# The weight sums of a seven-product matrix multiply: from VectorE to transfers that add

## The reference, cut to what matters

```
h = rms_norm(x, norm_ffn)
gate, up = jnp.split(h @ w_gate_up, 2, axis=-1)      # 1024 -> 2 x 2816
x = x + (jax.nn.silu(gate) * up) @ w_down            # 2816 -> 1024
```

## Time and profile before

| | us |
|---|---|
| median of three runs | 1362.07 |
| lowest and highest | 1361.05, 1362.75 |
| the profiled execution, its own time | 1360.11 |
| its span in the trace | 1358.3 |

### The profile page before, as it was taken

How to read it: one execution, slowest core, us unless ns; L and a number is a source line. 1 busy time by engine, 2 the same in 40 slices (tenths; PEclk the granted TensorE clock), 3 DMA queues, 4 the chain that set the end, 5 groups by cost and what they waited for, 6 DMA issues and landing times. The chain is left out here.

```text
span 1358.3 us, 18018 instructions
## 1 busy us (share of the span) xinstructions
PE 1339.5 (99%) x6941; PEld 1112.0 (82%) x6941; DVE 849.2 (63%) x1313; ACT 619.4 (46%) x1145; POOL 54.1 (4%) x38
## 2 busy tenths in 40 slices
PE   9999999999999999999999999999999999999998
PEld 7888878888888888888788887888798888888886
DVE  5785654457666554344558876767565666666668
ACT  6554333457777533223426466663343332433333
POOL 0025300000000000000010000000000000000000
PEclk9999999999999999999999999999999999999999
DMA  5222213242111154322261200002325412421321
GB/s 168 86 83 81 67 59 114 88 138 80 36 59 61 63 188 151 104 91 66 87 195 61 70 17 16 32 1 78 130 88 168 142 38 87 154 94 63 113 73 62
DMA packets 33622, 120.68 MB, mean 89 GB/s; under 512 B 3716, under 2 KB 5124, under 8 KB 32258
## 3 DMA queue, kind: packets, MB, share of 16 engines
q1 hardware_dynamic: 32962, 118.48, 26.3%
q10 hardware_dynamic: 576, 1.05, 0.4%
HBM read 112.18 MB, written 4.19 MB: 86 GB/s over the span
## 5 line engine op out<-in xcount | busy, mean ns | idle before, releaser
L983 PE MATMUL bank<-a_hi,whi 128*128 128x512 f32 (+1 forms) x880 | 346.9, 394 | 0.4 <-DVE a_lo L2381 0.4
L983 PE MATMUL bank<-a_hi,wlo 128*128 128x512 f32 (+1 forms) x880 | 337.1, 383 | 0.0
L983 PE MATMUL bank<-a_lo,whi 128*128 128x512 f32 (+1 forms) x880 | 336.2, 382 | 0.0
L1431 ACT ACTIVATE whi<-wraw 128x1024 fp32r<-128x1024 f32 x170 | 176.0, 1055 | 195.6 <-PE bank L983 135.1
L1808 DVE TENSOR_TENSOR wlo<-wraw,whi 128x1024 fp32r<-128x1024 f32 x170 | 207.6, 1234 | 60.7 <-ACT whi L1431 54.7
L983 PEld LDWEIGHTS bank<-a_hi,wlo 128*128 128x128 f32 x880 | 165.5, 188 | 32.7
L983 PEld LDWEIGHTS bank<-a_hi,whi 128*128 128x128 f32 x880 | 165.9, 189 | 31.6 <-issue 2.3
L983 PEld LDWEIGHTS bank<-a_lo,whi 128*128 128x128 f32 x880 | 165.9, 189 | 31.1 <-issue 1.7
L983 PE MATMUL bank<-arena 128*128 128x128 f32 (+5 forms) x1332 | 184.9, 284 | 3.0 <-DVE arena L2032 1.5
L983 PEld LDWEIGHTS bank<-arena 128*128 128x128 f32 (+1 forms) x1332 | 163.9, 190 | 13.0 <-issue 5.3
L983 PE MATMUL bank<-whi,a_hi 128*128 128x512 f32 x288 | 115.6, 401 | 1.5 <-DVE wlo L1808 0.7
(11 more groups left out here) (272 smaller groups left out, 1866.5 us busy)
## 6 DMA issues: line engine op xcount, KB each, us to landing
wraw<-in_wblk SPq DMA_DIRECT2D x170, 512.0 KB, 3.8
arena<-in_quarters SPq DMA_DIRECT2D x8, 1024.0 KB, 7.1
arena<-in_quarters SPq DMA_DIRECT2D x4, 768.0 KB, 6.1
arena<-in_x SPq DMA_DIRECT2D x4, 512.0 KB, 6.1
arena<-in_x SPq DMA_DIRECT2D x1, 2048.0 KB, 7.7
spill<-arena SPq DMA_DIRECT2D x4, 512.0 KB, 7.8
arena<-spill SPq DMA_DIRECT2D x1, 2048.0 KB, 9.3
out<-arena SPq DMA_DIRECT2D x8, 256.0 KB, 2.0
```

What stands on the lines that cost most here:

```text
L983: return nc.tensor.matmul(o, lhsT, rhs, start=start, stop=stop, **kw)
L1431: A(whi[n % 2][:, cols], wraw[i][:, 0:cols.stop - cols.start], ACT.Copy).then_inc(s_hi, 1)
```

## The change

The scheme's signs are chosen anew, so that all four weight sums are plain sums: t1 = b11 + b12, t2 = b11 + b12 + b22, t3 = b12 + b22, t4 = t2 + b21. None is made on VectorE. SP copies one quarter into the sum's slot, and POOL issues transfers that add further quarters from HBM onto it: t1 one, t3 one, t2 two, the second after the first has landed. t4 has no slot of its own: b21 is added onto t2 in place, after both rests of product 6 have been made. There are six copies and five adds per group, 33 transfers of quarters where there were 12. The slots are b11 (later b22), b21, t2 (later t4), t1, t3. The copies go ahead of ff 4 (t2), 5 (t1, t3), 6 (b11), 7 (b21) in group 0, the same places of ff 12 to 15 in group 1, and ahead of ff 19 (t2, t1), 20 (t3, b11), 21 (b21) in group 2. b22 goes ahead of the second woven block of the next group (for the last group, after all block weights), and waits for the rests of product 1. From the second group on, the others wait for the rests of the product of the group before that used the slot last; for t2 that is product 4. In the hidden sums two operations change sign, and two takes subtract in place of one.

```diff
@@ -72,9 +72,11 @@
 PRODUCT_ORDER = (1, 2, 6, 5, 7, 3, 4)
 CONTINUES = (6, 7, 3)
 PAIR = {1: 0, 6: 0, 7: 0, 4: 0, 2: 1, 5: 1, 3: 1}
+SUBTRACTED = {(6, (0, 1)), (7, (1, 1))}
 TAKES = {1: ((0, 0),), 2: ((0, 0),), 6: ((0, 1),), 5: ((1, 1),), 7: ((1, 0), (1, 1)), 3: ((0, 1),), 4: ((1, 0),)}
-QUARTERS = ("b11", "b12", "b21", "b22")
-SUMS = ("t1", "t2", "t3", "t4")
+QUARTERS = ("b11", "b21", "b22", "t1", "t3", "t2")
+COPIED = {"b11": 0, "b21": 2, "b22": 3, "t1": 0, "t3": 1, "t2": 0}
+ADDED = {"t1": (1,), "t3": (3,), "t2": (1, 3)}
@@ -291,17 +293,14 @@
         woven = group + 1 < len(FFP)
         for c in range(max(a + 3 * (group > 0), 2), e):
             f = ff(c, a, whole)
-            sums = [("tsum", group, 0)] if c == e - 2 else []
-            steps += f[:2] + untaken + H(*unsplit) + f[2:4] + sums + f[4:]
+            steps += f[:2] + untaken + H(*unsplit) + f[2:]
             untaken, unsplit = [], [c]
-        steps[-2:-2] = [("tsum", group, 1)]
         made = products(group, (e - a) // 2)
         for p in PRODUCT_ORDER:
             m = next(made)
             if p == 1 and not woven:
                 untaken, unsplit = H(*unsplit), []
-            sums = {6: [("tsum", group, 2)], 7: [("tsum", group, 3)]}.get(p, [])
-            steps += m[:2] + untaken + m[2:-1] + sums + m[-1:]
+            steps += m[:2] + untaken + m[2:]
             untaken = [("take", m[0][1])]
             if woven and p in (1, 6, 7):
                 c = FFP[group + 1][0] + (1, 6, 7).index(p)
@@ -575,12 +574,16 @@
 OUT1 = sorted((g for g, (kind, _) in enumerate(TILES) if kind == "out1"), key=DONE.get)
 LATE = min(n for n, b in enumerate(BLOCKS) if TILES[b["tiles"][0]][0] == "z_sb") + 1
 LOADED = [n for n, b in enumerate(BLOCKS) if b["form"] != "product"]
-LAST_OF = {"b12": 7, "b22": 3, "b21": 4}
+LAST_OF = {"t1": 5, "t3": 7, "b11": 3, "b21": 2, "t2": 4}
 QUARTERS_AT = {}
 for group, (a, e) in enumerate(FFP):
-    for c, name in zip(range(e - 4, e) if e - a == 8 else (e - 3, e - 3, e - 2, e - 1), ("b11", "b12", "b22", "b21")):
+    for c, name in zip((e - 4, e - 3, e - 3, e - 2, e - 1) if e - a == 8 else (e - 3, e - 3, e - 2, e - 2, e - 1),
+                       ("t2", "t1", "t3", "b11", "b21")):
         n = next(n for n, b in enumerate(BLOCKS) if TILES[b["tiles"][0]] == ("ff_gate", (c, c - a)))
         QUARTERS_AT.setdefault(n, []).append((group, name))
+    if group + 1 < len(FFP):
+        n = next(n for n, b in enumerate(BLOCKS) if TILES[b["tiles"][0]] == ("ff_gate", (e + 1, 1)))
+        QUARTERS_AT.setdefault(n, []).append((group, "b22"))
 PRODUCT_AT = {(b["group"], b["product"]): n for n, b in enumerate(BLOCKS) if b["form"] == "product"}
 MERGE_AFTER = max(n for n, b in enumerate(BLOCKS) if b["w"] == "gate_sb")
 TURNS = [s for s in SPLITS if s[0] in ("turn", "nsa", "chunk")]
@@ -756,8 +759,8 @@
         hsq = mem(4, [512])
-        raw = {name: mem(kb, [BLK]) for name, kb in (("b11", 0), ("b12", 8), ("b21", 16), ("b22", 24), ("t1", 32))}
-        raw.update(t2=raw["b11"], t3=raw["b12"], t4=raw["b21"])
+        raw = {name: mem(kb, [BLK]) for name, kb in (("b11", 0), ("b21", 8), ("t2", 16), ("t1", 24), ("t3", 32))}
+        raw.update(b22=raw["b11"], t4=raw["t2"])
         half_chunk = T // 2
         first_hi, first_lo = [mem(kb, [4, half_chunk], rounded_arena) for kb in (40, 44)]
         other_hi, other_lo = [mem(kb, [2, 4, half_chunk], rounded_arena) for kb in (52, 60)]
@@ -841,7 +844,7 @@
         s_qk2, s_k2 = sem("s_nsa_stacks_rounded"), sem("s_nsa_keys_twice")
         s_kcl = sem("s_kc_rest")
         s_raw = {name: sem("s_quarter_" + name) for name in QUARTERS}
-        s_tsum = sem("s_weights_summed")
+        s_added = {name: sem("s_quarter_added_" + name) for name in (*ADDED, "t4")}
         s_h, s_hsum, s_hround = sem("s_hidden_made"), sem("s_hidden_summed"), sem("s_hidden_rounded")
         s_hlb, s_hlev = sem("s_lower"), sem("s_hgrn_operands")
@@ -901,6 +904,20 @@
         @block.sync
         def _(sp):
             by_token = lambda ap: ap.rearrange("(a p) d -> p a d", p=P)
+            def load_quarter(group, name):
+                if name == "b22":
+                    sp.wait_ge(s_lo, 2 * PRODUCT_AT[group, 1] + 2)
+                elif group == 0:
+                    sp.wait_ge(s_norm, norm_no("ffn", NT - 1))
+                    sp.wait_ge(s_split, max(SPLITS.index(x) for x in SPLITS if x[:2] == ("turn", "ffn")) + 1)
+                else:
+                    sp.wait_ge(s_lo, 2 * PRODUCT_AT[group - 1, LAST_OF[name]] + 2)
+                cols = slice(0, width(PRODUCT_AT[group, 1]))
+                src = dram["quarters"][4 * group + COPIED[name]]
+                sp.dma_start(raw[name][:, cols], src[:, cols]).then_inc(s_raw[name], 16)
             for t in range(NT):
                 if t == 1:
                     sp.dma_start(cst[:, :], dram["cst"]).then_inc(s_ident, 16)
@@ -908,16 +925,7 @@
             sp.dma_start(swraw[:, 0:NK * SH], dram["w_dt"]).then_inc(s_sw, 16)
             for at, n in enumerate(LOADED):
                 for group, name in QUARTERS_AT.get(n, ()):
-                    if group == 0:
-                        sp.wait_ge(s_norm, norm_no("ffn", NT - 1))
-                        sp.wait_ge(s_split, max(SPLITS.index(x) for x in SPLITS if x[:2] == ("turn", "ffn")) + 1)
-                    elif name == "b11":
-                        sp.wait_ge(s_tsum, len(SUMS) * group)
-                    else:
-                        sp.wait_ge(s_lo, 2 * PRODUCT_AT[group - 1, LAST_OF[name]] + 2)
-                    cols = slice(0, width(PRODUCT_AT[group, 1]))
-                    src = dram["quarters"][len(QUARTERS) * group + QUARTERS.index(name)]
-                    sp.dma_start(raw[name][:, cols], src[:, cols]).then_inc(s_raw[name], 16)
+                    load_quarter(group, name)
                 for i in range(2):
                     if n >= 1:
                         sp.wait_ge(s_lo, 2 * LOADED[at - 1] + i + 1)
@@ -969,6 +977,7 @@
                     sp.wait_ge(s_spill, 16 * NT)
                     sp.dma_start(x2, by_token(spill)).then_inc(s_back, 16)
                     sp.dma_start(rows["ffn"], dram["norm_ffn"]).then_inc(s_row["ffn"], 16)
+            load_quarter(len(FFP) - 1, "b22")
             for p, (rows_half, cols_half) in ((2, (0, 0)), (7, (1, 1)), (3, (0, 1)), (4, (1, 0))):
                 for t in range(2):
                     sp.wait_ge(*ended(tile_of("down", (len(FFP) - 1, p, t))))
@@ -1421,10 +1430,10 @@
                 cols = piece(n, i)
                 if BLOCKS[n]["form"] == "product":
                     group, name = BLOCKS[n]["group"], PRODUCTS_OF[BLOCKS[n]["product"]][1]
-                    if name in QUARTERS:
+                    if name in COPIED and name not in ADDED:
                         act.wait_ge(s_raw[name], 16 * group + 16)
                     else:
-                        act.wait_ge(s_tsum, len(SUMS) * group + SUMS.index(name) + 1)
+                        act.wait_ge(s_added[name], 16 * len(ADDED.get(name, "1")) * (group + 1))
                     A(whi[n % 2][:, cols], raw[name][:, cols], ACT.Copy).then_inc(s_hi, 1)
                     return
                 act.wait_ge(s_w[i], 16 * (LOADED.index(n) + 1))
@@ -1949,32 +1958,14 @@
                 a12, a22 = h[:, 0:half_chunk], h[:, half_chunk:T]
                 dve.wait_ge(s_h, c + 1)
                 v.tensor_tensor(hsum[:, 2, :], a11, a21, ALU.subtract)
-                link(v.tensor_tensor(hsum[:, 0, :], a21, a22, ALU.add))
+                link(v.tensor_tensor(hsum[:, 0, :], a21, a22, ALU.subtract))
                 link(v.tensor_tensor(hsum[:, 1, :], hsum[:, 0, :], a11, ALU.subtract))
-                v.tensor_tensor(hsum[:, 3, :], a12, hsum[:, 1, :], ALU.subtract).then_inc(s_hsum, 1)
+                v.tensor_tensor(hsum[:, 3, :], a12, hsum[:, 1, :], ALU.add).then_inc(s_hsum, 1)
                 dve.wait_ge(s_hround, rounded_of_h(c) - 1)
                 v.tensor_tensor(other_lo[:, :, pair, :], h.rearrange("p (a b) -> p a b", b=half_chunk),
                                 f32(other_hi[:, :, pair, :]), ALU.subtract).then_inc(s_split, 1)
                 dve.wait_ge(s_hround, rounded_of_h(c))
                 v.tensor_tensor(sums_lo[:, :, pair, :], hsum, f32(sums_hi[:, :, pair, :]), ALU.subtract).then_inc(s_split, 1)
-
-            def tsum(group, i):
-
-                cols = slice(0, width(PRODUCT_AT[group, 1]))
-                r = {name: ap[:, cols] for name, ap in raw.items()}
-                out_, left, right = (("t1", "b12", "b11"), ("t2", "b22", "t1"), ("t3", "b22", "b12"), ("t4", "t2", "b21"))[i]
-                for name in (left, right):
-                    if name in QUARTERS:
-                        dve.wait_ge(s_raw[name], 16 * group + 16)
-                    else:
-                        dve.wait_ge(s_tsum, len(SUMS) * group + SUMS.index(name) + 1)
-                if out_ == "t3":
-                    dve.wait_ge(s_tsum, len(SUMS) * group + 1)
```

(28 more changed lines are left out.)

## The result

The changed kernel takes 1386.8 us (median of four runs, 1384.5 to 1387.2) against 1361.6 for the kernel before (1359.7 to 1362.8, four runs beside it): ratio 1.0185, 95% interval 1.0172 to 1.0198. It is 25 us slower. The forecast was 1366.9, with a range up to 1380: the right sign, a fifth of the size.

What follows compares the result with a forecast made beforehand. TensorE was taken as the bound, busy 1339.5 of 1358.3 us. Block 19's wait 3.55, first add 0.8, block 20 0.5, less 0.1 gained, made +4.8 us on the 1362.07 median: 1366.9 us, range 1364.5 to 1380.

Steps and rivals of the forecast that it cites:

- The bound and the gain: Whole kernel: TensorE bounds it; removing twelve VectorE sums (25.3 us) gains 0.1 us, at most 2.0 us.
- The pause near 1328: Last group, before the matmul at 1329.85: 1.9 us, caused by the hidden split after block 21, not the sums; stays.
- The wait for product 4 in front of block 19: Group 2, SP's queue: t2's wait for product 4's last rest delays block 19's weights; stall 3.55 us.
- The 0.8 us for the first add: Group 2, block 19: t2's first add slows the first weight piece; 0.8 us taken, bounds 0 to 2.5 us.
- hidden, with little to spare: Group 0, weights up to block 6: copies 18.4 us plus four adds 13.4 us fill 32 of 34 us; no stall.
- Group 1's "hidden": Group 1: t2's copy waits until about 1158, before block 12's weights, issued 1162.25 and wanted at 1176; no stall.
- rival 2: SP's queue: adds cost 5.0 us each and starve weights; 16.4 us in group 2, up to 11 each in groups 0, 1; chance 0.24.
- Weights must land 2.5 us before: Group 0, block 6 beginning near 1073: its weights must land some 2.5 us before its start.
- Blocks 20 and 21: Group 2 after block 19: block 20 stalls 0.5 us, bounds 0 to 2.8; block 21 has a whole block more.
- The margin of 2.2 us for block 20: Group 2: block 20's first piece lands at 1300.7, wanted at 1302.9, against up to two adds of 2.5 us each.
- 2.45 us from landing to start: Feed-forward blocks 19 and 20: 2.35 us from rounding to first rest, plus 0.1 us to notice the landing.
- the forecast's +4.8: Whole kernel, net slowdown in us: 3.55 + 0.8 + 0.5 - 0.1, all stalls in group 2; bounds +1.5 to +8.9.

Runs made afterwards that it cites:

- both cures: Changed kernel with group 0, 1 and group 2's t2 adds after the last feed-forward weights, and group 2's t2 and t3 copies swapped: 1361.0 us, ratio 1.0003.
- the last three runs: both cures (1361.0 us); the last hidden chunk's split one slice later on top of them (1359.8 us); that split move alone in the kernel before (1358.9 us).

## Why the prediction was wrong

**The bound and the gain: right.** TensorE was the bound; 23 us less of VectorE bought nothing that shows (ratio 1.0003 once the transfers are out of the way). The pause near 1328 stayed, 1.94 us, and its cause was the one named: moving the hidden split shortened it, removing the sums did not.

**The wait for product 4 in front of block 19: right in place and size.** Forecast 3.55 us, measured 3.66 without adds (3.72 with the adds moved away) and 3.90 with them. The 0.8 us for the first add came to 0.24 at most, one trace against another: POOL issued it at 1304.56, a quarter of a microsecond after t2 had landed, and the first piece of block 19 still took only 8.1 us.

**Groups 0 and 1, "hidden, with little to spare": the step that failed.** It summed 18.4 us of copies and 13.4 us of adds into 34, at the price of a copy for both and with the whole queue at 314 GB/s. An add costs 1.9 times a copy in engine time, and two or three in flight beside SP's queue leave it 101 GB/s. At the measured 5.09 us per MB the four adds are 21.4 us in place of 13.4, and the prediction's own sum becomes 39.8 us in a space of 34: the price of the add alone turns "hidden" into "late". The sum also watched block 6; the block that came late was 5, in the middle of the 34 us. Group 1's "hidden" left its adds out altogether.

The prediction kept the dearer add as rival 2. Its price held in kind (5.09 us per MB, 4.0 us for 0.79 MB where it said 5.0); that the slot is read is its reason, which no run shows apart from the sum. The adds did not go before the copies, but they held the engines 73% of the time while both queues were full. What groups 0 and 1 would add under it was priced (up to 11 us each) and left outside the range, at a chance of 0.06; they added 11.3 us together. In group 2, where rival 2 had 16.4 us, the pauses were 8.2.

The Trainium skill's rule, Collectives: The Full Stack, "The bandwidth ceiling: the fold count and why AG ≠ RS ≠ AR", that an adding transfer reads two sources and runs at half the rate, agrees in its rate with the runs: 5.09 against 2.65 us per MB. The prediction had it in a sentence, and took the copy's price for the sum. The rule of the Trainium skill, DMA: Bandwidth & Descriptors, "Queues, rings and completion order", that engines take turns between queues by packets, fits too: 199 packets of one queue and 195 of the other in the 10 us in which both were full.

**"Weights must land 2.5 us before": too short for block 5.** Its first piece landed at 1064.3, and TensorE started at 1069.36, 5 us later. ACT, in order, held the roundings of the hidden split behind the weights it waited for, and VectorE does that split ahead of the weights' rest. The timeline of VectorE:

```profile
1065.95 0.69 DVE L1965 TENSOR_TENSOR rounded_arena<-arena,rounded_arena 128x512 fp32r<-128x512 f32 x1 [11.33 <-ACT rounded_arena L1536]
1066.90 1.23 DVE L1968 TENSOR_TENSOR b_lo<-arena,b_hi 128x1024 fp32r<-128x1024 f32 x1 [0.26 <-ACT b_hi L1538]
1068.04 1.22 DVE L1817 TENSOR_TENSOR wlo<-wraw,whi 128x1024 fp32r<-128x1024 f32 x1
```

The prediction did not name what is queued behind ACT's wait for the weights; here it was 2.5 us of the 7.0.

**Blocks 20 and 21: under the upper bound, over the value taken.** 2.3 and 2.1 us of pause for 0.5 and 0. Block 20's pieces, issued from 1311.3 on, had t2's first add beside them, block 21's the three adds that POOL issued at 1316.5 (the second of t2, t1's, t3's); the pieces took 7.6 to 8.6 us to land. The margin of 2.2 us for block 20 rested on the same 2.45 us from landing to start. In the trace its first piece is rounded at 1319.00, VectorE makes a whole hidden split first, and its rest comes at 1325.03:

```profile
1319.00 1.06 ACT L1440 ACTIVATE whi<-wraw 128x1024 fp32r<-128x1024 f32 x1 [7.76 <-DMA wraw<-in_wblk]
```

```profile
1320.40 0.42 DVE L1954 TENSOR_TENSOR rounded_arena<-arena,rounded_arena 128x256 fp32r<-128x256 f32 x1 [6.71 <-ACT rounded_arena L1534]
...
1325.03 1.22 DVE L1817 TENSOR_TENSOR wlo<-wraw,whi 128x1024 fp32r<-128x1024 f32 x1
```

From landing to TensorE's start at 1326.34 that is 7.4 us, not 2.45. The kernel with copies alone has the same 7.3 us there (landed at 1299.6, the rest done at 1306.9), behind a landing 5.6 us after the issue, and no pause; with the adds the landing came 2.0 us later, and the pause was 2.3.

**The clock: missing altogether.** 5.0 us more of matmul time. The granted clock is 0.70 in the 5 us behind block 5's pause, 0.62 and 0.59 in the 4 us behind those of blocks 13 and 19. No term of the sum and no rival had it. The trace before could not show it: its single pause of 1.94 us left the clock at 1.00. The same pause in the kernel with both cures did not, as the last section's rows show, so a pause of this length sometimes costs clock and sometimes none, and one of 3.7 us did each time.

Taken together, the forecast's +4.8 became 8.2 us of pauses in group 2, 11.3 in groups 0 and 1, and 5.0 of slow matmuls: 24.5.

## What to carry to other kernels

Work that leaves an idle engine for the transfer engines is free only where these have room within the slack of the transfers that the bound waits for: sum it window by window, with the adding transfer at its own price, and put it where the other queue is empty. Here the same adds cost 20 us in one place (1386.8 against 1366.3; 19 by the ratios) and nothing measurable 20 to 40 us later. Count the slack from the landing to the matmul along every engine in between, in its own order: it was 2.5 us for block 19, 5 for block 5 and 7.4 for block 20. When a load is put behind a new wait in a queue, shift the old rows by the time of the wait: the stall came out 0.11 us from the forecast without adds, 0.35 with them. And a TensorE pause of some 4 us costs more than itself: in the 8 us behind one, where the full clock has 35 matmuls (the changed kernel from 1074.31 on, at 1.00), there were 23 in the kernel with copies alone and 28 behind those of 3.9 and 4.3 us in the changed kernel, so 2.7 and 1.6 us by 0.227 us each.

## What was not expected of the hardware

- An adding transfer from HBM onto a slot took 5.09 us of the 16 engines per MB, a plain one by the same queue 2.65. Nearly alone, an add of 1024 KB landed 8.1 us after its issue and one of 768 KB after 7.3, where SP's copies in the same trace took 4.7 and 4.3 at best.
- Issuing it cost POOL 0.86 us, a plain copy 0.53.
- In the kernel with copies alone, after 3.66 us without a matmul, the granted clock stood at 0.50 for 4 us and returned to 1.00 within 8; 2.5 us of matmul time.
- The old pause of 1.94 us has two outcomes. The window of 4 us behind it, first in the kernel with copies alone, then in the one with both cures:

```profile
1335.90:1339.90 4.00, 4.00 (x17) 3.27 (x18) 3.67 (x6) 0.00 (x0) 0.00 (x0) 1.00 0.00 0
```

```profile
1330.41:1334.41 4.00, 4.00 (x12) 3.14 (x13) 3.43 (x5) 0.00 (x0) 0.27 (x1) 0.64 0.00 0
```

  17 matmuls in one, 12 in the other, the work and the pause ahead of them the same; the 108 matmuls from there on take 25.00 us in one and 26.53 in the other. The scatter between executions fits it: of the 27 of the kernel before beside the last three runs, the 8 with a mean clock of 0.997 took 1362.1 to 1363.2 us, the other 19 (0.998 and more) 1359.0 to 1361.7; with the split moved in the kernel before, which leaves 0.70 us of the pause, none of 11 is at 0.997. What decides between the two stays open.
- Adds and copies changed nothing in the 316.24 us run of matmuls beside them: no contention with TensorE showed.
